# Two attention layers of a fused six-layer kernel: an unscaled copy, rotary products read from PSUM, moved evictions, copies moved from VectorE to ScalarE, and weight splits placed earlier

## The reference, cut to what matters

```python
def rope(x, pos):
    ...
    x1, x2 = xf[..., :half], xf[..., half:]
    out = jnp.concatenate([x1 * cos - x2 * sin, x2 * cos + x1 * sin], axis=-1)
...
def dsa_mixer(xn, positions, w_in, q_norm, k_norm, w_out):
    q, k, v, z, qi, ki, wi = jnp.split(xn @ w_in, cuts, axis=-1)
    q = rope(rmsnorm(q.reshape(bsz, seq, B_HEADS, B_HEAD_DIM), q_norm), positions)
    k = rope(rmsnorm(k.reshape(bsz, seq, B_HEADS, B_HEAD_DIM), k_norm), positions)
    ...
    wi = wi * (IDX_HEADS ** -0.5 * IDX_DIM ** -0.5)
    ...
        rel = jax.nn.relu(jnp.einsum("qhd,sd->qhs", qi_b, ki_b).astype(jnp.float32))
        score = jnp.einsum("qh,qhs->qs", w_b.astype(jnp.float32), rel)
        ...
        top_val, top_idx = lax.top_k(score, topk)
        ...
        p = jax.nn.softmax(logits, axis=-1).astype(v_sel.dtype)
    ...
    return (o * jax.nn.silu(z)) @ w_out

def mla_mixer(xn, positions, w_in, q_lat_norm, kv_lat_norm, w_uq, w_ukv, q_norm, k_norm, w_out):
    cq, ckv, kr, z = jnp.split(xn @ w_in, cuts, axis=-1)
    q = (rmsnorm(cq, q_lat_norm) @ w_uq).reshape(bsz, seq, C_HEADS, C_QK)
    kv = (rmsnorm(ckv, kv_lat_norm) @ w_ukv).reshape(bsz, seq, C_HEADS, C_NOPE + C_V)
    ...
    o = dense_chunk_attention(q, k, v, C_QK ** -0.5).reshape(bsz, seq, C_WIDTH)
    return (o * jax.nn.silu(z)) @ w_out
```

## Time and profile before

| What | Value |
|---|---|
| Median of 3 runs | 966.38 us (965.67 to 966.61) |
| Profiled execution | 965.7 us |
| Its span in the trace | 964.1 us |
| Mean granted clock of TensorE | 0.991 of full |
| Busy: PE, PEld, DVE, ACT, POOL | 94%, 89%, 68%, 52%, 33% of the span |
| Chain that ended last | PE 60%, DVE 10%, ACT 6%, POOL 3% of the span |

### The profile page before, as it was taken

How to read it: one execution, slowest core, us unless ns; L and a number is a source line. 1 busy time by engine, 2 the same in 40 slices (tenths; PEclk the granted TensorE clock), 3 DMA queues, 4 the chain that set the end, 5 groups by cost and what they waited for, 6 DMA issues and landing times.

```text
span 964.1 us, 16784 instructions
## 1 busy us (share of the span) xinstructions
PE 907.5 (94%) x6761; PEld 853.6 (89%) x6761; DVE 651.7 (68%) x1011; ACT 498.3 (52%) x712; POOL 322.0 (33%) x266
## 2 busy tenths in 40 slices
PE   6999999988899996999999997999999999999986
PEld 5999997767789985889999997999999998988986
DVE  5786666999686788776776657777646645555642
ACT  5634355554685676675443353353535336575631
POOL 7533322462121334233343138864103000223330
PEclk9999999999999999999999999999999999999999
DMA  9885546244314432256695534345664652524401
GB/s 250 210 219 175 181 143 212 88 150 172 116 58 146 137 117 108 88 141 161 176 227 192 176 131 175 100 163 182 221 252 144 215 175 88 175 88 175 180 18 45
DMA packets 123585, 148.70 MB, mean 154 GB/s; under 512 B 9561, under 2 KB 79102, under 8 KB 123518
## 3 DMA queue, kind: packets, MB, share of 16 engines
q1 hardware_dynamic: 121472, 145.63, 46.8%
q10 hardware_dynamic: 1582, 1.12, 0.4%
q0 software_dynamic: 464, 1.02, 0.3%
HBM read 146.70 MB, written 1.05 MB: 153 GB/s over the span
## 4 chain that ended last, share of the span: by engine, by line
PE 60%; DVE 10%; ACT 6%; POOL 3%; issue 2%; ACTq 0%; POOLq 0%; DVEq 0%
PE acc L1693 43%; PE aux L1693 16%; DVE wlo L892 3%; POOL arena L1553 1%; ACT work L681 1%; POOL arena L1554 1%; ACT arena L508 1%; POOL arena L1552 1%; ACT work L679 1%; DVE arena L994 1%; DVE score L1146 1%; ACT work L695 1%; DVE sqy L1083 1%; DVE top L1145 1%; DVE work L1209 0%
## 5 line engine op out<-in xcount | busy, mean ns | idle before, releaser
L892 DVE TENSOR_TENSOR wlo<-raw,whi 128x2048 fp32r<-128x2048 f32 (+5 forms) x115 | 276.6, 2432 | 85.7 <-ACT whi L474 83.9
L1693 PE MATMUL acc<-xh,whi 128*128 128x256 f32 x1128 | 323.8, 287 | 10.3 <-DVE wlo L911 5.1
L1693 PE MATMUL acc<-xl,whi 128*128 128x256 f32 x1128 | 321.2, 285 | 0.0
L1693 PE MATMUL acc<-xh,wlo 128*128 128x256 f32 x1128 | 321.1, 285 | 0.0
L474 ACT ACTIVATE whi<-raw 128x2048 fp32r<-128x2048 f32 (+5 forms) x115 | 197.3, 1744 | 78.6 <-PE acc L1693 38.1
L1693 PEld LDWEIGHTS acc<-xh,whi 128*128 128x128 f32 x1128 | 218.0, 193 | 12.6 <-issue 8.4
L1693 PEld LDWEIGHTS acc<-xl,whi 128*128 128x128 f32 x1128 | 218.2, 193 | 0.0
L1693 PEld LDWEIGHTS acc<-xh,wlo 128*128 128x128 f32 x1128 | 218.2, 193 | 0.0
L1617 POOL CAST yh<-ytmp 128x256 fp32r<-128x256 f32 x24 | 24.3, 1011 | 216.9 <-DVE ytmp L1455 123.3
L1693 PE MATMUL acc<-whi,xh 128*128 128x512 f32 (+1 forms) x208 | 81.6, 392 | 6.3 <-DVE arena L994 2.9
L1693 PE MATMUL aux<-yh,whi 128*128 128x256 f32 x288 | 82.2, 286 | 0.0
(11 more groups left out here) (339 smaller groups left out, 1732.4 us busy)
## 6 DMA issues: line engine op xcount, KB each, us to landing
raw<-in_a_w_in SPq DMA_DIRECT2D x52, 512.0 KB, 6.7
raw<-in_sb_w_in SPq DMA_DIRECT2D x48, 512.0 KB, 5.5
raw<-in_b_w_in SPq DMA_DIRECT2D x36, 512.0 KB, 5.3
raw<-in_pool_w_in SPq DMA_DIRECT2D x32, 512.0 KB, 5.9
raw<-in_a_w_out SPq DMA_DIRECT2D x16, 512.0 KB, 4.8
raw<-in_pool_w_out SPq DMA_DIRECT2D x16, 512.0 KB, 4.9
raw<-in_sb_w_out SPq DMA_DIRECT2D x16, 512.0 KB, 5.0
raw<-in_b_w_out SPq DMA_DIRECT2D x8, 512.0 KB, 5.1
```

The costliest lines, as they stand in the source:

```text
L892: TT(wlo[b][:, lo:hi], (raw_third if third else raw[b])[:, lo:hi], whi[b][:, lo:hi].bitcast(F32), ALU.subtract).then_inc(lo_ready, 1)
L1693: return nc.tensor.matmul(out_, lhsT, rhs, start=start, stop=stop, skip_group_check=True)
```

## The change

1. In the sparse layer ACT's two copies of qi (token_raw of unit B0) are written ahead of first_half(B0+2) and of the root of the norm, and are without the factor rT. The factor goes into wi: DVE multiplies it by rT and by the constant, in two instructions in place of one (L1112).
2. The turned products of q and k (not of qi) read acc in PSUM, times rT (SCALAR_TENSOR_TENSOR, L1099 of the changed kernel), in place of the SBUF copy. PE waits for tok_turn before it writes that part of acc again.
3. turn_at of B0+5 stands at k = 7, was k = 5.
4. ACT's eviction of vB for B0+8 stands ahead of the exponentials of j = 2, was behind them.
5. Sparse softmax: parts of B0+9 are fillers 5 to 8 (were 5, 6, 8, 9), output parts 10 to 13 (were 11 to 14), quarters of B0+10 are split at j = 2, 3 and of B0+11 at 5, 6 (were one j later). silu of z stands at j = 4, in the latent layer at j = 3 (both were 5).
6. Latent layer: of the turn copies DVE has 1, 3, 5, 7, ACT all others; the banks of groups 12 to 15 alternate between acc 1 and acc 0. DVE's copies 5 and 7 stand ahead of q_factor(0). Quarters 0 and 1 of C0+7 are split ahead of the softmax, quarters 2 and 3 at j = 0. Parts of C0+7 are fillers 1, 3, 5, 6 (were 3, 5, 6, 8), output parts 9, 11, 12, 13 (were 11 to 14), the splits of C0+8 and C0+9 one j earlier.

```diff
@@ -256,7 +256,13 @@
                 return (aux[:, 0, :], aux[:, 1, :], acc[:, 2, :], acc[:, 3, :])[i % 4]
-            return (acc[:, 1, :], acc[:, 2, :], acc[:, 3, :], acc[:, 1, :])[i - 12]
+            return acc[:, 1 - i % 2, :]
+
+        def turned_out(i):
+
+            if i % 2 and i < 8:
+                return "turn_out_v", i // 2 + 1
+            return "turn_out_a", i // 2 + 1 if i < 9 else i - 3
@@ -314,8 +320,8 @@
 
-        SPARSE_SPLITS = {**quarters(B0 + 9, (0, 1)), **quarters(B0 + 10, (3, 4)), **quarters(B0 + 11, (6, 7))}
-        MLA_SPLITS = {**quarters(C0 + 7, (0, 1)), **quarters(C0 + 8, (3, 4)), **quarters(C0 + 9, (6, 7))}
+        SPARSE_SPLITS = {**quarters(B0 + 9, (0, 1)), **quarters(B0 + 10, (2, 3)), **quarters(B0 + 11, (5, 6))}
+        MLA_SPLITS = {0: ((C0 + 7, 2), (C0 + 7, 3)), **quarters(C0 + 8, (2, 3)), **quarters(C0 + 9, (5, 6))}
         FILLERS = (("v", 1), ("z", 1), ("z", 2), ("v", 2), ("z", 3), ("v", 3))
@@ -573,6 +579,9 @@
 
+            act.wait_ge(unit_done, B0 + 1)
+            for t in range(NT):
+                A(raw_slot(t), acc[:, t, :], ACT.Copy).then_inc(sem("tok_raw"), 1)
             first_half(B0 + 2)
@@ -608,7 +617,6 @@
             act.wait_ge(sem("rt_ready"), 2)
-            token_raw(0)
             act.wait_ge(unit_done, B0 + 2)
@@ -672,6 +680,8 @@
                 for j in range(HEADS // 2 + 1):
+                    if layer == 0 and j == 2:
+                        values(vB, B0 + 8, 1, 1)
                     for i in (2 * j, 2 * j + 1):
@@ -683,10 +693,9 @@
                         nc.scalar.preload_act_table_set("natural_log_exp_and_others")
-                    if layer == 0 and j == 2:
-                        values(vB, B0 + 8, 1, 1)
                     if layer == 1 and j < 2:
                         turn_copy(12 + 2 * j)
+                        turn_copy(13 + 2 * j)
                     if j:
@@ -696,7 +705,7 @@
                         split_quarter(u, q)
-                    if j == 5:
+                    if j == 4 - layer:
                         silu(44 if layer else 28, 4, 4 if layer else 2)
@@ -795,7 +804,11 @@
             turn_copy(8)
+            turn_copy(9)
+            split_quarter(C0 + 7, 0)
             turn_copy(10)
+            split_quarter(C0 + 7, 1)
+            turn_copy(11)
             softmax_heads(1)
@@ -1077,11 +1090,16 @@
                         dve.wait_ge(sem("tok_done"), j - 1)
-                    raw, turn = by_head(raw_slot(j)), by_head(turn_slot(j))
+                    raw = by_head(acc[:, 2 * (TOKEN_UNITS[e] % 2) + t, :] if e else raw_slot(j))
+                    turn = by_head(turn_slot(j))
                     sin = idx_tab[:, 1, t, :] if e == 0 else qk_tab[:, 1 - e % 2, 1, t, :]
-                    TT(turn[:, :, 0:n], raw[:, :, n:2 * n], over_heads(sin[:, 0:n]), ALU.mult)
-                    TT(turn[:, :, n:2 * n], raw[:, :, 0:n], over_heads(sin[:, n:2 * n]), ALU.mult)\
-                        .then_inc(sem("tok_turn"), 1)
+                    for lo, other in ((0, n), (n, 0)):
+                        to, of, by = turn[:, :, lo:lo + n], raw[:, :, other:other + n], over_heads(sin[:, lo:lo + n])
+                        if e:
+                            ins = STT(to, of, rT[:, 4 + t:5 + t], by, ALU.mult, ALU.mult)
+                        else:
+                            ins = TT(to, of, by, ALU.mult)
+                    ins.then_inc(sem("tok_turn"), 1)
@@ -1109,7 +1127,9 @@
             dve.wait_ge(sem("ki_raw"), 2)
-            me.link(TS(wi[:, :, :], wi[:, :, :], float(8 ** -0.5 * 64 ** -0.5), None, ALU.mult))
+            for t in range(NT):
+                ins = TS(wi[:, t, :], wi[:, t, :], rT[:, 4 + t:5 + t], float(8 ** -0.5 * 64 ** -0.5), ALU.mult, ALU.mult)
+            me.link(ins)
             TT(ki_b[:, :, 0:16], kis[:, :, 16:32], idx_tab[:, 1, :, 0:16], ALU.mult)
@@ -1221,13 +1241,9 @@
                 for j in range(HEADS // 2 + 2):
-                    if j == 5:
-                        take(C0 + 7 if layer else B0 + 9, 44 if layer else 28, "z_raw")
                     if j < HEADS // 2:
...
                         minima(2 * j + 1)
-                    if layer == 1 and j < 2:
-                        turn_copy(13 + 2 * j)
                     if j >= 2:
@@ -1238,6 +1254,8 @@
                         q_factor(1)
+                    if j == 4 - layer:
+                        take(C0 + 7 if layer else B0 + 9, 44 if layer else 28, "z_raw")
@@ -1351,11 +1369,11 @@
                     turn_copy(3)
-            q_factor(0)
             turn_copy(5)
             turn_copy(7)
-            turn_copy(9)
-            turn_copy(11)
+            q_factor(0)
+            split_quarter(C0 + 7, 0)
+            split_quarter(C0 + 7, 1)
             softmax_heads(1, mask, 40)
@@ -1924,12 +1942,16 @@
             taken("tok_raw", 4)
+            taken("tok_turn", 4)
             token_unit(B0 + 4, index_last)
             taken("tok_raw", 6)
-            token_unit(B0 + 5, turn_at({5: 2}))
+            taken("tok_turn", 6)
+            token_unit(B0 + 5, turn_at({7: 2}))
             taken("tok_raw", 8)
+            taken("tok_turn", 8)
             token_unit(B0 + 6, turn_at({4: 3}))
             taken("tok_raw", 10)
+            taken("tok_turn", 10)
             unit(B0 + 7, in_tiles(1), xh, xl, turn_at({6: 4}))
@@ -1951,19 +1973,19 @@
                     v_unit(B0 + 8, 1, 2 * f, 2)
-                if f in (5, 6, 8, 9):
+                if 5 <= f < 9:
                     if f == 5:
                         taken("v_ready", 4)
-                    unit(B0 + 9, in_tiles(1), xh, xl, part=(2 * (5, 6, 8, 9).index(f), 2))
+                    unit(B0 + 9, in_tiles(1), xh, xl, part=(2 * (f - 5), 2))
                 out_filler(f, 0)
...
 
-                u, y0 = (C0 + 8, 16) if layer else (B0 + 10, 8)
-                if f == 11:
+                u, y0, at = (C0 + 8, 16, (9, 11, 12, 13)) if layer else (B0 + 10, 8, (10, 11, 12, 13))
+                if f == at[0]:
                     taken("z_raw", 2 * layer + 2)
-                if 11 <= f < 15:
-                    attention_out(u, y0, f - 11, 0)
+                if f in at:
+                    attention_out(u, y0, at.index(f), 0)
                 if 15 <= f < 17:
@@ -1990,19 +2012,18 @@
                     turn_heads(13 + f)
-                if f in (3, 5, 6, 8):
-                    if f == 3:
-                        taken("turn_out_v", 8)
-                        taken("turn_out_a", 8)
-                    unit(C0 + 7, in_tiles(1), xh, xl, part=(2 * (3, 5, 6, 8).index(f), 2))
+                if f in (1, 3, 5, 6):
+                    if f == 1:
+                        taken(*turned_out(11))
+                    unit(C0 + 7, in_tiles(1), xh, xl, part=(2 * (1, 3, 5, 6).index(f), 2))
                 out_filler(f, 1)
...
                 if 4 <= i < 12:
-                    taken("turn_out_v" if i % 2 else "turn_out_a", (i - 4) // 2 + 1)
-                elif i > 12:
-                    taken(*((), ("turn_out_a", 6), ("turn_out_v", 6), ("turn_out_a", 7))[i - 12])
+                    taken(*turned_out(i - 4))
+                elif i >= 14:
+                    taken(*turned_out(i - 2))
                 g = i % 8 // 4
@@ -2018,9 +2039,7 @@
                         if layer == 1:
-                            taken("turn_out_v" if j % 2 else "turn_out_a", (8 + j) // 2 + 1)
-                            if j == 0:
-                                taken("turn_out_v", 5)
+                            taken(*turned_out(max(8 + j, 9)))
                         for i in (2 * j, 2 * j + 1):
@@ -2032,6 +2051,8 @@
                             taken("v_ready", 2 + t // 2)
+                        if layer == 1 and t == 0:
+                            taken(*turned_out(15))
                         for n, (c, p) in enumerate(((0, slice(0, T)), (P, slice(T, W384)))):
...
                                 o = acc[64 * (h % 2):64 * (h % 2) + 64, 0, T * (t % 2):T * (t % 2) + T]
```

## The result

The changed kernel takes 955.69 us (median of 4 runs, 955.19 to 956.76) against 966.5 for the kernel before on the same chip. The ratio is 0.9891, with a 95% interval from 0.9874 to 0.9908. The forecast was 957.2, in a range from 954.0 to 961.0. A second set of runs of the same kernel gave 955.43.

A forecast was written before the change was run, and what follows sets the result against it. PE was taken as the bound, busy 907.5 of 964.1 us. Gains of 1.6 + 3.7 + 2.8 + 3.2 = 11.3 us gave 955.1 at full clock; one half-clock spell of 2.1 made it 957.2, range 954.0 to 961.0.

The forecast's parts named there:

- Bound and places: Whole kernel: PE bounds it; eight PE waits, 20.9 us together, all touched by the change, nothing outside the two layers.
- Copy of qi first: Start of B0+2: PE no longer waits 2.48 us for ACT's copy; gain 1.6 us, bounds 1.0 and 1.9.
- Turned products: Token units: products reading PSUM are free of POOL's holds; PE gains 3.7 us, bounds 0.7 and 4.8.
- the wlo rows unchanged: Sign for the token units: DVE's low halves of weights keep their durations while products take 0.46 to 0.49 us.
- an overhead of reading PSUM: DVE's quoted access overhead, about 125 ns on PSUM against 60 on SBUF; estimated 1.0 us for sixteen products.
- vB and the sparse softmax: Sparse softmax: earlier eviction gains 4.6 us, new waits for silu and later PVs cost 1.8; net 2.8, bounds 1.5 and 4.
- Latent layer: Latent layer: 8.9 us gained, new waits of 1.25, 1.2 and 3.4 lost; net 3.2, bounds 1 and 5.
- case 2: The forecast: one half-clock spell at the latent layer's PV3 costs 2.1 us, 957.2 us; chance 0.36.
- case 3: The clock also falls at 371 to 375 in the latent layer, costing 3.0 us more, 960.2 us; chance 0.10.
- the row that I chose by, 255: Sparse softmax before the change: clock fell after a 2.99 us wait, taken as the model for PV3's 3.4 us wait.
- Case 4: Token units: POOL holds wlo instead, or PSUM reads don't free DVE; gain 0.7, time 958.1 or 960.2; chance 0.12.
- Case 7: Latent layer: slower if the load for quarter 0 of C0+7 lands late; landing at 385 gives 971; chance 0.03.

The follow-up runs named there:

- u_qi: Changed kernel with the copies of qi behind the root again, with the factor rT, and wi multiplied once: 956.5 us.
- u_turn: Changed kernel with the turn of tokens in B0+5 at k = 5 again: 954.94 us.
- u_vb: Changed kernel with ACT's eviction of vB behind the exponentials of j = 2 again: 959.14 us.
- x_fill: Changed kernel with the sparse softmax's fillers, quarters, silu and take as before, the eviction of vB staying in front: 952.35 us.
- u_psum: Changed kernel with the turned products of q and k read from SBUF again, the later turn kept: 959.79 us.

## Why the forecast came out

**Bound and places.** Seven of the eight places read in the earlier trace rows changed, and behind the last latent PV nothing did. The eighth, the take of z, stayed (1.80, now 1.82), as the token paragraph says and the first one ("all eight") does not. This step holds.

**Copy of qi first.** Taken 1.6, bounds 1.0 and 1.9; u_qi shows 1.67. PE starts at 146.47 (forecast 146.5), 1.99 earlier from rT than in u_qi, and a new wait of 0.59 at 157.15, for the ki chain, takes part of it back.

**Turned products.** Taken 3.7 for the token units, bounds 0.7 and 4.8; measured 6.53 - 1.67 = 4.86. The duration was right (0.476 against 0.472 from the earlier trace rows), so was the freedom from POOL seen in the earlier trace rows. The mis-sized term is what comes late next: I left 2.3 us of waits (1.0 for the low half, 1.0 at the turn in B0+6, 0.3), and there are 0.59, none, 0.51 and 0.35. The rest of the 1.16 is small waits. What the step left out is that a product no longer held also frees the low half behind it (3.37 to 2.83 and 2.82). Its sign "the wlo rows unchanged" failed by this, and B0+8 came at 230.5, ahead of the 231 to 232. The 1.00 that DVE waited for POOL was not given back: it is 1.67 now. That the later turn "covers what POOL is still late" was an empty step beside the products: u_turn shows 0.00.

The 0.054 that a product costs more at rest came out (0.058). But the prediction sets it beside an overhead of reading PSUM, as if the two were one thing, and they are not. Three lines of the kernel before, by the same query as the earlier trace rows, the first reading PSUM, the others SBUF alone:

```profile
L1024 DVE TENSOR_TENSOR arena<-acc,r x16: 417/418/420, 35.7 to 536.5; 128x256 f32<-128x256 f32 x16
```

```profile
L1035 DVE TENSOR_TENSOR arena<-arena x16: 417/418/421, 42.8 to 544.6; 128x256 f32<-128x256 f32 x16
```

```profile
L1030 DVE SCALAR_TENSOR_TENSOR arena<-upad,G,arena x16: 483/485/487, 39.5 to 541.2; 128x256 f32<-128x256 f32 x16
```

TENSOR_TENSOR takes 0.418 from either memory, and SCALAR_TENSOR_TENSOR 0.485 from SBUF and 0.472 from PSUM (L1404). In these rows the extra goes with SCALAR_TENSOR_TENSOR, the instruction that multiplies by rT as well, and not with PSUM. These rows show no price of reading PSUM, so the overhead that the prediction quotes for it isn't borne out here, and that the two sums, 1.0 by that overhead and 0.9 by the rows, lay close together is luck.

**vB and the sparse softmax.** Taken 4.6 - 1.8 = 2.8; measured 2.81. Both halves hold by themselves: 4.65 by u_vb (4.49 beside the old table, 56.77 - 52.28), and 1.68 lost by the table in x_fill. The reason beside the 1.8 was right too, silu not ready at output part 0 (1.4 forecast, 1.50 read). What I missed is what follows from it: the forecast held an edit with a loss of its own, and my later expectation in x_fill, that the table pays for itself, was wrong.

**Latent layer.** Taken 3.2 at full clock, less 2.1 for one spell: 1.1; measured 1.21. This is right by two errors. The new waits were sized well (1.25, 1.2 and 3.4 as matmul idle; read 1.16, 1.23 and 3.52), and the cause of the longest was right. ACT ahead of the copies for PV3, in the changed kernel:

```profile
387.72 2.01 ACT L488 ACTIVATE whi<-raw 128x1024 fp32r<-128x1024 f32 x2
389.75 1.28 ACT L676 ACT_TABLE_LOAD   x1
391.04 1.06 ACT L676 ACTIVATE arena<-arena 128x1024 f32<-128x1024 f32 x1
392.12 1.28 ACT L710 ACT_TABLE_LOAD   x1
...
395.55 0.84 ACT L704 ACTIVATE work<-aux 128x384 f32<-128x384 f32 x2
```

silu with its two loads takes 3.65 (forecast 3.67) and stands ahead of two heads of exponentials. Mis-sized were the old waits that went. The sum has 0.2 for all small terms, but three waits that it doesn't list, in the kernel before

```profile
374.29 1.18 PEld L1693 LDWEIGHTS aux<-arena 96*128 96x128 f32 x8 [0.62 <-DVE stat L1213]
...
411.11 0.63 PEld L1693 LDWEIGHTS acc<-work,vC 128*64 128x64 f32 x8 [1.00 <-ACT work L695]
...
417.77 0.63 PEld L1693 LDWEIGHTS acc<-work,vC 128*64 128x64 f32 x8 [1.18 <-ACT work L695]
```

became one of 0.72 at 412.03. So with no spell at all the gain would be 132.53 - 127.90 = 4.6, not 3.2. Against that stood two spells, 3.4 us, not one of 2.1.

**The clock.** The forecast was case 2, one spell. The profile shows case 3's spell at 365 as well, with a price of 1.71 where I took 3.0. In the second profile it is one place, with twice the loss. At PV3 the row that I chose by, 255, was right: all eight profiles with that wait of 3.9 have a spell there. The price was not: it is 1.71 or 3.4, not 2.1. At 365 no row decides: the same waits gave a spell in one execution and none in the next. And the split of the rows into softmax and dense work doesn't hold, since u_psum has a spell behind 3.61 in dense work.

**Rivals.** Case 4 (hold stays) is excluded by the sixteen at 0.476; its half-truth is that the low half and POOL's add still hold each other, though the low half less than before. Case 7 (late load of C0+7) did not occur: ACT's quarter 0 began at 360.10, without idle time of its own.

**Sum.** 5.3 + 2.8 + 1.1 = 9.2 forecast, 6.5 + 2.8 + 1.2 = 10.5 measured. The 1.3 is nearly all the token term. That the other two come out to 0.1 is by terms that were right in the sparse layer and by errors that cancel in the latent one.

## What to carry to other kernels

Where VectorE and GpSimd work side by side, let VectorE read an operand from PSUM while it is still there: sixteen products fell from 0.76 to 0.48 us on average. When a table of fillers is moved forward to meet work that comes earlier, undo it once by itself, because here it cost 1.68 us inside a change that gained, and two tables set anew took 4.6 us of waits out. When one edit frees an engine, look for what stood behind it: here the low halves gained with the products, and the later turn lost its worth. Add up PE's waits in stretches between fixed instructions and count half-clock windows apart, or a clock spell will be read as an effect of an edit.

## What the runs showed of the hardware that was not expected

Half-clock spells lose 1.71 us or twice that (3.39 to 3.42), nothing between, in all profiles read here at the two layers. Behind waits of 2.99, 3.08, 3.61, 3.92 and 5.34 us there was one in every profile that has the wait, behind one of 3.06 among dense products there was none, and at the pair of 1.56 and 1.45 it came in some executions only. With 28 matmuls whose result nobody reads in a wait of 3.9, the clock stayed up in the one profile taken, and the latent layer was 1.3 us shorter. A VectorE instruction reading one input from PSUM took as long as from SBUF alone (0.418 us for 128x256), and was not held by GpSimd. A hold between the two engines does not vanish when one of VectorE's instructions leaves it: POOL's adds went from 14.8 to 18.2 us in sum, beside low halves that got shorter.
